# Attention queries and keys transposed by VectorE in blocks and moved by DMAs, instead of transposed by TensorE

## The reference

```
q = (rms_norm(c_q) @ w_uq)            # 256 x (8 heads x (64 nope + 32 rope))
q_rope, k_rope = rotary(...)          # the 32 rope columns; k_rope is shared by the heads
k_nope, v = c_kv_n @ w_uk, c_kv_n @ w_uv
s = (q_nope @ k_nope.T + q_rope @ k_rope.T) / sqrt(96)    # causal
y_attn = softmax(s) @ v @ w_attn_o
merged = g0 * y_attn + g1 * y_conv + g2 * y_pool          # g: 6 x 512 gate columns, sigmoid
y = rms_norm(merged @ w_mix_o)
```

## Time and profile before

| | us |
|---|---|
| median of 3 runs | 793.99 (793.89 to 794.09) |
| profiled execution: own time | 794.23 |
| its span, first to last instruction | 792.4 |
| TensorE busy | 784.0 |
| VectorE busy | 567.6 |
| ScalarE busy | 427.6 |
| GpSimd busy | 78.2 |

### The profile page before, as it was taken

How to read it: one execution, slowest core, us unless ns; L and a number is a source line. 1 busy time by engine, 2 the same in 40 slices (tenths; PEclk the granted TensorE clock), 3 DMA queues, 4 the chain that set the end, 5 groups by cost and what they waited for, 6 DMA issues and landing times.

```text
span 792.4 us, 10213 instructions
## 1 busy us (share of the span) xinstructions
PE 784.0 (99%) x3740; PEld 661.7 (84%) x3740; DVE 567.6 (72%) x814; ACT 427.6 (54%) x604; POOL 78.2 (10%) x111
## 2 busy tenths in 40 slices
PE   8999999999999999999999999999999999999997
PEld 7998888888888888888889888888888888888885
DVE  6688999879675666654476979996896755556553
ACT  6577565564564454454475666556545545445441
POOL 1620000113210000000221100002203000000000
PEclk9999999999999999999999999999999999999999
DMA  9675444536567666676355654444564676666641
GB/s 357 225 247 164 156 160 134 185 125 192 171 234 229 215 210 207 210 249 208 130 201 170 223 176 133 145 150 160 166 213 167 228 223 210 226 208 213 208 156 54
DMA packets 51729, 151.26 MB, mean 191 GB/s; under 512 B 9776, under 2 KB 14896, under 8 KB 51680
## 3 DMA queue, kind: packets, MB, share of 16 engines
q1 hardware_dynamic: 51280, 148.93, 56.6%
q0 software_dynamic: 256, 1.16, 0.4%
q10 hardware_dynamic: 144, 0.52, 0.2%
HBM read 143.77 MB, written 1.05 MB: 183 GB/s over the span
## 4 chain that ended last, share of the span: by engine, by line
PE 98%; DMA 1%; ACT 0%; DVE 0%; DVEq 0%; POOLq 0%; issue 0%; SPq 0%; POOL 0%; ACTq 0%
PE acc L438 28%; PE acc L440 28%; PE acc L439 28%; PE acc L557 7%; PE tp L512 3%; PE misc L719 1%; PE tp L737 1%; PE tp L524 1%; DMA gates<-x_cols 1%; PE misc L679 0%; PE tp L695 0%; PE misc L439 0%; PE misc L438 0%; PE misc L440 0%; PE misc L681 0%; ACT w_hi L858 0%
## 5 line engine op out<-in xcount | busy, mean ns | idle before, releaser
L1189 DVE TENSOR_TENSOR w_lo<-raw,w_hi 128x1024 fp32r<-128x1024 f32 (+2 forms) x246 | 299.1, 1227 | 128.3 <-ACT w_hi L858 127.6
L858 ACT ACTIVATE w_hi<-raw 128x1024 fp32r<-128x1024 f32 (+2 forms) x252 | 258.6, 1039 | 167.6 <-PE acc L440 161.1
L438 PE MATMUL acc<-w_hi,xT_hi 128*128 128x512 f32 (+2 forms) x692 | 268.2, 388 | 0.0
L440 PE MATMUL acc<-w_hi,xT_lo 128*128 128x512 f32 (+2 forms) x692 | 264.9, 383 | 0.0
L439 PE MATMUL acc<-w_lo,xT_hi 128*128 128x512 f32 (+2 forms) x692 | 264.7, 383 | 0.0
L440 PEld LDWEIGHTS acc<-w_hi,xT_lo 128*128 128x128 f32 x692 | 129.9, 188 | 24.8
L439 PEld LDWEIGHTS acc<-w_lo,xT_hi 128*128 128x128 f32 x692 | 130.0, 188 | 23.9
L438 PEld LDWEIGHTS acc<-w_hi,xT_hi 128*128 128x128 f32 x692 | 130.0, 188 | 23.6
L438 PE MATMUL acc<-w_hi,hT_hi 128*128 128x512 f32 (+1 forms) x300 | 117.3, 391 | 0.0
L440 PE MATMUL acc<-w_hi,hT_lo 128*128 128x512 f32 (+1 forms) x300 | 116.2, 387 | 0.0
L439 PE MATMUL acc<-w_lo,hT_hi 128*128 128x512 f32 (+1 forms) x300 | 116.1, 387 | 0.0
(11 more groups left out here) (147 smaller groups left out, 638.9 us busy)
## 6 DMA issues: line engine op xcount, KB each, us to landing
raw<-weights SPq DMA_DIRECT2D x247, 512.0 KB, 3.7
raw<-weights SPq DMA_DIRECT2D x14, 384.0 KB, 3.8
gates<-gates SPq DMA_DIRECT2D x160, 32.0 KB, 2.5
raw<-weights SPq DMA_DIRECT2D x8, 288.0 KB, 4.1
gain<-gains SPq DMA_DIRECT2D x4, 512.0 KB, 6.4
x_sb<-x_rows SPq DMA_DIRECT2D x2, 512.0 KB, 9.5
out_rows<-x_sb SPq DMA_DIRECT2D x4, 256.0 KB, 2.0
const<-consts POOLq DMA_DIRECT2D x1, 896.0 KB, 7.9
```

What stands on the lines that cost most here:

```text
L438: pe.matmul(out, a_hi, b_hi, start=start, stop=False)
L440: return pe.matmul(out, a_lo, b_hi, start=False, stop=stop)
L858: ins = act.activation(w_hi[:, s, first:end], raw[:, s, first:end], ACT.Copy, scale=by)
L1189: ins = dve.tensor_tensor(w_lo[:, s, 0:width], raw[:, s, 0:width], f(w_hi[:, s, 0:width]), ALU.subtract)
```

## The change

TensorE's transposes of queries and keys go, and with them their copies from PSUM. VectorE transposes queries and keys in 32 x 32 blocks (`turn_heads`): for each 32 columns c of the 96, one instruction over both token tiles and all heads. A block transposed that way still stands on the partitions of its token quarter q; a DMA of 32 partitions x 512 numbers (64 KB) per c and q moves it to partitions 32c to 32c + 31. There are 12 for queries and 12 for keys in each layer. The queries land in `placed_q`, and ScalarE copies them to `q_t` in four instructions so that a head's 128 tokens are in one run. The keys land in `u_hc` and are read from there by the scores, in runs of 32. The query transfers and half of the key transfers are on GpSimd's queue, the other half on SP's, behind the load of unit 30.

```diff
-TP = ([... "CKV0", "CKV1", "Q0", "Q1", "Q2", "Q3", "K0", "K1", "K2", "K3",
+TP = ([... "CKV0", "CKV1",
...
+        q_t = gates[:, :, 2 * D:3 * D].rearrange("p t (h s) -> p t h s", h=HEADS)
+        k_t = u_hc[:, :, :, :].rearrange("p b c (t h j) -> p (b c) t h j", t=TOK, h=HEADS)
+        turned_q = [gates[:, i // 2, 512 * (i % 2):512 * (i % 2 + 1)] for i in range(QK // BLK)]
+        turned_k = [gates[:, 0, D:D + 512], gates[:, 1, D:D + 512], gates[:, 0, D + 512:2 * D]]
+        placed_q = [qk_flat[:, 512 * i:512 * (i + 1)] for i in range(QUADS - 1)] + [gates[:, 1, 512:1024]]
...
+        def move_keys(eng, l, part):
+            for h in range(2):
+                eng.wait_ge(misc_full[h], l * 2 + 1)
+            for i in range(HEAD_MOVES // 2 * part, HEAD_MOVES // 2 * (part + 1)):
+                c, q = divmod(i, QUADS)
+                eng.wait_ge(k_turned, l * (QK // BLK) + c + 1)
+                eng.dma_start(u_hc[BLK * c:BLK * (c + 1), q // 2, q % 2, :], turned_k[c][BLK * q:BLK * (q + 1), :]
+                              ).then_inc(k_in[part], 16)
...  SP's queue, after load(l, u, ...)
+                    if u == U_GATE + 5:
+                        move_keys(sp, l, 1)
...  TensorE: q_transposes and k_transposes and their calls are gone; in scores(n)
-                    if n == 0 or n == 4:
-                        for k in range(2):
-                            tp_emptied(pe, l, TPN["K0"] + n // 2 + k)
+                    if n == 0:
+                        pe.wait_ge(q_stored, QUADS * (l + 1))
+                        for half_in in k_in:
+                            pe.wait_ge(half_in, 16 * (HEAD_MOVES // 2) * (l + 1))
...
-                        mm = pe.matmul(misc[:, n % 2, i * keys:(i + 1) * keys], q_t[h // 4][0:QK, h % 4, tokens(t)],
-                                       k_t[h // 4][0:QK, h % 4, 0:keys], start=True, stop=True)
+                        for k in range(t + 1):
+                            mm = pe.matmul(misc[:, n % 2, i * keys + k * P:i * keys + (k + 1) * P],
+                                           q_t[0:QK, t, h, :], k_t[0:QK, :, k, h, :], start=True, stop=True)
...  ScalarE: store_T and its eight calls are gone; behind the high parts of units 29 and 30, two calls each
+                def store_q(q):
+                    act.wait_ge(q_in, 16 * HEAD_MOVES * (l + 1))
+                    src = placed_q[q][0:QK, :].rearrange("p (t h j) -> p t h j", t=TOK, h=HEADS)
+                    act.activation(q_t[0:QK, :, :, q * BLK:(q + 1) * BLK], src, ACT.Copy).then_inc(q_stored, 1)
...  VectorE
+                def turn_heads(src, dst, done):
+                    v = src[:, :, :].rearrange("p t (h d) -> p t h d", h=HEADS)
+                    for c in range(QK // BLK):
+                        dve.transpose(dst[c].rearrange("p (t h j) -> p t h j", t=TOK, h=HEADS),
+                                      v[:, :, :, c * BLK:(c + 1) * BLK]).then_inc(done, 1)
                 los(23, 24)
-                taps(3)
+                dve.wait_ge(q_roped, l + 1)
+                turn_heads(q_sb, turned_q, q_turned)
                 los(24, 25)
...  rope of the keys
                 taps(3)
-                for u in range(25, 29):
+                los(25, 26)
+                taps(3)
+                dve.wait_ge(k_roped, l + 1)
+                dve.wait_ge(k_nope, (l + 1) * TOK)
+                turn_heads(k_sb, turned_k, k_turned)
+                los(26, 27)
+                taps(2)
+                for u in range(27, 29):
                     lo(u)
-                    taps(3)
+                    taps(5)
...  GpSimd, behind the norms
+                pool.wait_ge(q_turned, (l + 1) * (QK // BLK))
+                for c in range(QK // BLK):
+                    for q in range(QUADS):
+                        pool.dma_start(placed_q[q][BLK * c:BLK * (c + 1), :], turned_q[c][BLK * q:BLK * (q + 1), :]
+                                       ).then_inc(q_in, 16)
+                move_keys(pool, l, 0)
```

More of the change, by code:

```diff
@@ L47 @@
 QUADS = P // BLK
+HEAD_MOVES = QUADS * (QK // BLK)
 POOL_LO = {(l, u) for l in range(LAYERS) for u in (U_FFN, U_FFN + 1)}
@@ L88, in fulls @@
     return len([u for u in upto if pair == 0 or u not in WIDE])
-TP = (["X0", "X1", "X2", "X3", "HC0", "HC1", "CQ0", "CQ1", "CKV0", "CKV1", "Q0", "Q1", "Q2", "Q3", "K0", "K1", "K2", "K3",
+TP = (["X0", "X1", "X2", "X3", "HC0", "HC1", "CQ0", "CQ1", "CKV0", "CKV1",
        "MT0", "MT1", *(f"{piece}{n}" for n in range(8) for piece in "PV"), "O0", "O1",
@@ L96 @@
 T_USES = len(TP)
-HI_OF = [n for n in TP if n[:2] != "HC" and n[0] not in "PQKV"]
+HI_OF = [n for n in TP if n[:2] != "HC" and n[0] not in "PV"]
 MUL_OF = [n for n in TP if n[0] in "XF"]
@@ L168, in build @@
         par = sb("par", [P, LAYERS, NPAR])
-        hc = sb("hc", [P, TOK, CONV])
         sg = sb("sg", [P, TOK, 512])
-        u_sb = sb("u_sb", [P, TOK, 512])
+        u_hc = sb("u_hc", [P, 2, TOK, 512])
         hcT = sb("hcT", [P, CT, TAPS - 1 + SEQ])
@@ L201, in build @@
         pooled = sg[:, :, :].rearrange("p t n -> p (t n)").rearrange("p (g n) -> p g n", g=4)
-        q_t = [gates[:, hh, 2 * D:3 * D].rearrange("p (h s) -> p h s", h=4) for hh in range(2)]
-        k_t = [buf[:, :, :].rearrange("p t n -> p (t n)").rearrange("p (h s) -> p h s", h=4)
-               for buf in (u_sb, hc)]
+        u_sb, hc = u_hc[:, 0], u_hc[:, 1]
+        q_t = gates[:, :, 2 * D:3 * D].rearrange("p t (h s) -> p t h s", h=HEADS)
[3 more added lines that the diff above has]
+        placed_q = [qk_flat[:, 512 * i:512 * (i + 1)] for i in range(QUADS - 1)] + [gates[:, 1, 512:1024]]
         rope_a, rope_b = hc[:, 0, :], hc[:, 1, :]
@@ L274, in build @@
         k_nope = sem("k_nope")
+        q_turned = sem("q_turned")
+        k_turned = sem("k_turned")
+        q_in = sem("q_in")
+        q_stored = sem("q_stored")
+        k_in = [sem(f"k_in{i}") for i in range(2)]
         conv_dve = sem("conv_dve")
@@ L655, in _ @@
                 col_group(U_POOL, 4, 2, 512, 1, "POOL", XT)
[L657 to L664, removed]
                 for t in range(TOK):
@@ L683, in _ @@
                     mm.then_inc(misc_full[h], 1)
-                q_transposes(1)
                 col_group(U_V, 1, 2, 512, 1, "V", HT, kt0=H_CKV)
@@ L697, in pool_products @@
                         mm.then_inc(tp_full[n % 2], 1)
[L699 to L705, removed]
                 def scores(n):
@@ L753, in attention @@
                 def attention(i):
-                    if i < 2:
-                        for n in range(TOK):
-                            k_transposes(2 * i + n)
                     s_n, p_n, v_n = after_gate(i)
@@ L1016, in _ @@
                                    ACT.Copy).then_inc(misc_free[h], 1)
-                store_q(1)
                 his(27, 28)
@@ L1073, in _ @@
                     if i < 2:
-                        for n in range(2 * i, 2 * i + 2):
-                            store_T(f"K{n}", k_t[i][0:QK, :, tokens(n % 2)])
+                        store_q(2 * i)
+                        store_q(2 * i + 1)
                     s_n, p_n, _ = after_gate(i)
```

## The result

The changed kernel takes 787.43 us (median of 6 runs) where the kernel before took 794.13 in the same set: ratio 0.9916, 95% interval 0.9905 to 0.9927. The forecast was 787.3. The profiled execution took 787.39 us. One execution of each kernel in the set took far longer, 1613.21 us before and 2149.93 after, for a reason that no trace shows, and the ratio leaves these two out.

The account below looks back on a forecast made before the run. TensorE's own instruction stream was taken as the bound. From 794.0 us, -7.0 for transposes, +0.1 for scores and +0.2 for VectorE's lag gave 787.3, its own range 786.3 to 788.3, the full range reaching up to 793.0.

Parts of the forecast that it names:

- The mechanism: TensorE's own instructions are the chain; a microsecond taken out is a microsecond gained, as long as no producer becomes late.
- TensorE's 64 transposes, -6.96: Query and key transposes leave TensorE: four pairs of groups per layer at 0.87 us, 3.48 per layer, 6.96 in all.
- Scores, +0.1 within 0 to 0.2: Second token tile's scores: one matmul on 256 keys becomes two on 128, costing 0.1 us, between 0 and 0.2.
- the bound of 10.6 us: Rival that strided keys slow the scores, up to 10.6 us if each column took twice as long: 794 to 798, chance 0.02.
- The sum: All priced terms off 794.0: -7.0 for transposes, +0.1 for scores, +0.2 for VectorE's stall, giving 787.3 us.
- VectorE's lag: Block transposes make VectorE late for the first scores' mask, at 86.3; priced as a 0.2 us stall, bounds 0 and 2.
- the named place: Layer 0's second score step: exponentials end at 96.3, TensorE reaches the transposes of probabilities at 96.0.
- Transfers: Query and key transfers before the first scores at 81.3: issues 0.63 us apart, keys 2.0 us early, queries 2.7, cost 0.
- rival 2: VectorE holds up GpSimd's DMA issues, 1.5 us each, stalling the first scores of both layers: 811.7 us, chance 0.12.
- Rival 1: GpSimd's 18 issues and their landing come late for the first scores, up to 4.6 us: 788 to 793, chance 0.17.
- the 0.95 us per issue: GpSimd's time per transfer issue above which the two layers' stalls exceed 6.7 us and the kernel ends slower than before.
- GpSimd at 0.81 us an issue: Slow end for the transfers, with 5.7 us to land: stalls of 2.9 us in layer 0 and 1.7 in layer 1, 791.9.

Follow-up runs that it names:

- e1: Changed kernel with the turning, the transfers and ScalarE's query copies left out, scores made from whatever lies in the buffers: 787.03 us.
- e2: Changed kernel with only keys turned by VectorE and moved by transfers, queries transposed by TensorE as before: 790.73 us.
- e6: Changed kernel with the second token tile's scores in one matmul per head on 256 keys, read in runs of 32: 786.97 us.
- e4: Changed kernel with 12 extra 64 KB query transfers per layer to unused places, issued on GpSimd's queue before the real ones: 804.34 us.
- e11: Changed kernel with e4's 12 extra query transfers per layer, each made 2 KB instead of 64 KB: 803.62 us.
- e5: Changed kernel with all 24 transfers a layer on SP's queue, none on GpSimd's: 791.53 us.
- e3: Changed kernel with VectorE turning the keys twice, three more block transposes per layer ahead of the real ones: 790.29 us.
- e10: Changed kernel with five more semaphores that nothing uses: 787.32 us.

## Why the prediction was right, point by point

- *The mechanism.* Held. TensorE's own instructions were the chain, the transposes came off it, and what replaced them is hidden but for 0.3 us (e1); the keys' half gives half (e2).
- *TensorE's 64 transposes, -6.96.* Mis-sized: they were worth 7.19, 0.90 for each group instead of the 0.87 that its piece of the chain shows. The other 0.03 lies outside that piece.
- *Scores, +0.1 within 0 to 0.2.* Mis-sized and outside its own bounds: +0.34, 0.04 for each of the eight wide steps. The pieces themselves are 0.89 instead of 0.87, +0.16; the rest again lies outside them. e6 takes all of it back in layer 1. Runs of 32 cost nothing (e6), so the bound of 10.6 us was far off, as the chance of 0.02 said.
- *The sum.* -6.96 + 0.1 + 0.2 = -6.7 was forecast and -6.74 measured, as -7.19 + 0.34 + 0.11. That the two agree to hundredths is luck: the 0.23 missing from the gain and the 0.24 missing from the price cancel.
- *VectorE's lag.* Mask of the first scores at 85.68, forecast 86.3. Block transposes follow each other at 0.605 us, not 0.645, which a row with the length of two at once does not show; that is 6 x 0.04 = 0.24 of the 0.6. Where the rest comes from was not worked out. The stall came at the named place and was 0.11; the recorded 96.3 against 96.0 makes 0.3, of which 0.2 was taken.
- *Transfers.* In time, as forecast. GpSimd's issues followed each other at 0.49 us, not 0.63, beside a VectorE that was never idle: its two-input operations, which stretched GpSimd's arithmetic in the earlier trace rows, do not hold up its DMA issues. The Trainium skill's rule (GPSIMD Engine Reference, Specifications), on which rival 2 hung, applies to the one and not to the other. Queries were in place 2.0 us early (forecast 2.7).
- *What was mis-sized besides: the price of being late.* Rival 1 and rival 2 were priced by the wait alone, as was the 0.95 us per issue from which the gain is gone (by the prediction's own sum, 34 x - 26.6 = 6.7, it is 0.98). In e4 and e11 the granted clock fell with waits of 4.4 to 6.6 us, in one of e5's executions behind a wait of 2.24; late transfers also landed later (e4, e11), and each GpSimd transfer lengthens the drain at the end. e4's issues are late by 5.9 us in each layer and cost 16.9 in all: 11.0 of waits, some 4 of clock, 2 at the end. The cliff was therefore nearer than the prediction put it: GpSimd at 0.81 us an issue, to which it gave 791.9, would by e4 have ended above that, an estimate that no run tests. The forecast stood on the right side of it.

## What to carry to other kernels

On a kernel whose chain of waits is one engine's own instructions, price an edit by that engine's pieces in the chain, and then ask of each replacement one question: by how many microseconds does it come ahead of the instruction that needs it. Slack is to be found by moving things, not from busy shares: here 3.6 us of additional VectorE work per layer cost tenths, and 1.8 more cost 1.9 in the one layer and 0.8 in the other. A small margin on transfers is worth less than it looks: waits of 4.4 to 6.6 us were charged twice here, by their length and by some 2 us of clock each, and a wait of 2.24 was in one execution of five. And look at the program's last instructions before transfers are put on GpSimd: their number lengthens its drain, which is free only as long as it ends before the output has landed.

## What had not been expected of the hardware

- After a TensorE wait of 2.24 us the granted clock was 0.60 and 0.55 in the next two stretches of 2 us (e5, the profiled execution). With one of 6.6 us it fell before the wait was over and was half until some 4 us behind it (e4). After a wait of 1.38 us (e5, layer 1) and waits of 1.05 us and less (e3, from 80 to 100 us) it stayed at 1.00.
- A GpSimd DMA issue of 32 rows took 0.50 us, 0.49 apart, less than SP's 0.59.
- Transfers of 64 KB landed in 1.9 to 5.7 us in the changed kernel, and in up to 8.5 in e4, where three held-back weight loads are under way.
- GpSimd's drain at the program's end took 1.00 us after 4 GpSimd transfers, 3.94 after 40, 5.25 after 56 and 5.90 after 64, 0.08 for each, whatever their size and whatever the number of semaphores (e4, e11, e10). The program's last wait is 0.2 us up to 40 and 1.2 and 1.8 us beyond.
